# Attention scores with keys on partitions: weights no longer transposed, row sums on VectorE, heads chained

## The reference

```
scores = einsum('bqhd,bkhd->bhqk', q, k) / sqrt(64)
bias   = F[q] - F[k]                    # F = cumsum(log_sigmoid(f)), one row for each head
logits = where(key <= query, scores + bias, -inf)
y_b    = einsum('bhqk,bkhd->bqhd', softmax(logits), v)
gates  = sigmoid(x @ w_gate + b)        # 3 * 1024 columns, computed beside the attention
```

## Time and profile before

| | us |
|---|---|
| median of 3 runs | 1965.41 |
| profiled execution | 1961.69 |
| its span, first to last instruction | 1960.3 |
| TensorE busy with matmuls | 1913.3 (98%) |
| VectorE busy | 1124.5 (57%) |
| ScalarE busy | 706.6 (36%) |
| GpSimd busy | 435.0 (22%) |

### The profile page before, as it was taken

How to read it: one execution, slowest core, us unless ns; L and a number is a source line. 1 busy time by engine, 2 the same in 40 slices (tenths; PEclk the granted TensorE clock), 3 DMA queues, 4 the chain that set the end, 5 groups by cost and what they waited for, 6 DMA issues and landing times. The chain is left out here.

```text
span 1960.3 us, 30528 instructions
## 1 busy us (share of the span) xinstructions
PE 1913.3 (98%) x10560; PEld 1623.1 (83%) x10560; DVE 1124.5 (57%) x2133; ACT 706.6 (36%) x1081; POOL 435.0 (22%) x548
## 2 busy tenths in 40 slices
PE   7999999999999999999999999999999989999998
PEld 6878887888887888888888788888888878999997
DVE  4564235654245655646465665565645568777776
ACT  3121013021034555555555655455555541111110
POOL 2927930498000000000000000000000002222322
PEclk9999999999999999999999999999999989999999
DMA  7124225322432151231423515133142276555542
GB/s 190 67 86 118 86 86 196 63 107 107 139 109 93 49 139 54 80 110 47 138 68 87 175 48 139 62 87 109 49 128 66 91 251 209 170 173 171 174 118 86
DMA packets 103479, 221.68 MB, mean 113 GB/s; under 512 B 10936, under 2 KB 56680, under 8 KB 99816
## 3 DMA queue, kind: packets, MB, share of 16 engines
q1 hardware_dynamic: 89648, 161.41, 26.2%
q0 software_dynamic: 12608, 55.19, 10.1%
q10 hardware_dynamic: 1152, 4.19, 0.5%
HBM read 155.09 MB, written 65.08 MB: 112 GB/s over the span
## 5 line engine op out<-in xcount | busy, mean ns | idle before, releaser
L1386 PE MATMUL g_ps<-x_hi,w_lo 128*128 128x512 f32 x768 | 309.4, 403 | 0.0
L1386 PE MATMUL g_ps<-x_hi,w_hi 128*128 128x512 f32 x768 | 308.4, 402 | 0.0
L1302 DVE TENSOR_TENSOR pt_lo<-t_ps,pt_hi 128x512 fp32r<-128x512 f32 (+2 forms) x320 | 190.4, 606 | 138.2 <-ACT pt_hi L1208 137.8
L643 PE MATMUL tile_ps<-x_hi,w_hi 128*128 128x512 f32 x752 | 234.1, 393 | 11.2 <-DVE x_lo L362 11.2
L643 PE MATMUL tile_ps<-x_hi,w_lo 128*128 128x512 f32 x752 | 232.1, 390 | 0.0
L643 PE MATMUL tile_ps<-x_lo,w_hi 128*128 128x512 f32 x752 | 232.0, 390 | 0.0
L1386 PE MATMUL g_ps<-x_lo,w_hi 128*128 128x512 f32 x768 | 225.9, 410 | 3.9 <-PEq L1423 2.6
L1208 ACT ACTIVATE pt_hi<-t_ps 128x512 fp32r<-128x512 f32 (+2 forms) x320 | 170.4, 533 | 142.4 <-PE t_ps L1345 137.9
L1240 DVE CUSTOM_DVE_ANT_0 s_sb<-s_ps,f_row 128x512 f32<-128x512 f32 (+2 forms) x320 | 181.6, 604 | 35.1 <-PE s_ps L1334 34.4
L1116 POOL DMA_DIRECT2D mixT<-y_out x63 | 33.8, 536 | 748.1 <-DVE y_out L1254 748.1
L1345 PE MATMUL t_ps<-ident,s_sb 128*128 128x128 f32 x1088 | 172.1, 273 | 9.6 <-DVE pt_lo L1302 5.2
(11 more groups left out here) (276 smaller groups left out, 3537.4 us busy)
## 6 DMA issues: line engine op xcount, KB each, us to landing
w_lo_raw<-in_w_tiles SPq DMA_DIRECT2D x96, 512.0 KB, 3.6
gateT<-g_out SPq DMA_DIRECT2D x96, 256.0 KB, 3.0
gate<-gateT SPq DMA_DIRECT2D x64, 384.0 KB, 4.5
x_lo_raw<-in_xT SPq DMA_DIRECT2D x24, 512.0 KB, 8.4
qkvT<-zout SPq DMA_DIRECT2D x24, 512.0 KB, 3.2
silT<-zout SPq DMA_DIRECT2D x16, 512.0 KB, 2.7
k_ll<-qkvT POOLq DMA_DIRECT2D x16, 512.0 KB, 6.7
q_st<-qkvT POOLq DMA_DIRECT2D x16, 512.0 KB, 8.7
```

The lines of the kernel that those rows point to most:

```text
L643: last = pe.matmul(tile_ps[par][:, c * BANK:(c + 1) * BANK], w[par][:, k, :], x[:, k, c * BANK:(c + 1) * BANK], start=(k == 0 and j == 0), ...
L1302: dve.tensor_tensor(pt_lo[part], t_ps[n % 2][:, 0:keys].rearrange("p (k q) -> p k q", q=P), pt_hi[part].bitcast(F32), ALU.subtract).then_i ...
L1386: mm = pe.matmul(g_ps[c][:], w[j % 2][:, k, :], x[:, k, c * BANK:(c + 1) * BANK], start=(r == 0), stop=(r == 3 * KT - 1))
```

## The change

The block of 512 queries takes the place of the query tile, and keys are on partitions from the start. A head has 20 units (`UNITS`): query block b (0 to 3) and a pair of key tiles i; a diagonal unit has fewer columns.

- `scores_t` computes logits with the key tile as weight and up to 512 queries as moving operand, in two products: `k_hh` by `q_st`, and `kl2` by `q2`. `kl2` is the low part of k with four rows of ones beneath it; `q2` is the high part of q with four rows that hold minus the row's maximum, so the maximum is subtracted by the product. F[k] is now a bias of each partition (`neg_f`) of ScalarE's exponential, which reads PSUM and writes `p_raw`. A second set of 16 mask products for each head belongs to it.
- The maxima come from a separate pass, `score`, with queries on partitions as before but with one product (`q_st` by `k_hh`), 40 pieces for a head, with its 16 masks. VectorE runs the same custom instruction over them, in place in PSUM (`score_max`), and reduces four tiles at once; `max_row` transposes the maxima and `max_rows` writes them to `q2`.
- There are no transposes of weights. ScalarE and VectorE split `p_raw`, in SBUF, to `p_hi` and `p_lo`.
- Row sums: VectorE adds up `p_raw` over the key tiles in `acc` (`accumulate`), and `row_sums` does four plain float32 products with a column of ones for each query block; then the inverse and its transposes as before.
- `values` has 512 columns for each product in place of 256.
- Heads are chained: the product passes of the next head's blocks 0 and 1, its maxima, half of its v and its first unit are computed in the last steps of this one (`SCORE_STEPS`, `bank_uses`); keys and queries are split in steps 13, 15, 17 and 19. The first head does this work in `AHEAD`, with 32 fills. Scores, maxima, v, sums and inverses share two PSUM banks, `s_ps`.
- In the last head the split of the merge's first operand lies in the last steps; one copy of the head's code more stands in the program (first, phase 0, phase 1, last).

```diff
+UNITS = [(b, i) for b in range(4) for i in range(2 * b + 2)]
+SCORE_STEPS = {0: (14, (2, 2)), 1: (16, (1, 2, 2, 3)), 2: (0, (3, 4, 3, 2)), 3: (4, (2, 4, 3, 2, 3, 2))}
+MAX_STEP = {0: 16, 1: 0, 2: 4, 3: 10}
+V_STEP = {0: 16, 1: 2}
+SPLIT_STEP = (13, 15, 17, 19)
+FILL = (20, 13, 12, 15, 15, 13, 11, 16, 14, 13, 11, 9, 10, 17, 11, 17, 13, 18, 14, 17)
+FILL_TAIL = (3, 3, 3)
+FILL_AHEAD = (14, 10, 8)
...
         @block.scalar
+            def weights(at, n, first, ahead=0):
+                for s, k, q0 in tiles(n):
+                    act.wait_ge(st_full, at(2 * STEPS, 2 * (n + ahead * STEPS) + s + 1))
+                    act.activation(p_raw[n % 2][:, s, q0:], st_ps[:, s, q0:], ACT.Exp,
+                                   bias=neg_f[:, bass.ds(at(Q_TILES, k + ahead * Q_TILES), 1)]).then_inc(p_ready, 1)
...
+                if full(n):
+                    act.activation(p_hi[n % 2][:], p_raw[n % 2][:], ACT.Copy).then_inc(p_high, 1)
...
         @block.vector
-                    dve.tensor_tensor_reduce(s_sb[t % 2][:, k0:k0 + keys], s_ps[n % 3][:, 0:keys],
-                                             f_row[:, k0:k0 + keys], 1.0, -3e38, ALU.subtract, ALU.max,
-                                             mx[t % 2][:, j:j + 1]).then_inc(s_free, 1)
+                scores = s_ps[u % 2][:, 0:keys]
+                dve.tensor_tensor_reduce(scores, scores, f_row[:, j * BANK:j * BANK + keys],
+                                         1.0, -3e38, ALU.subtract, ALU.max, mx[:, t % 4, j:j + 1]).then_inc(s_free, 1)
...
+                        dve.wait_ge(accumulated, at(ACC, done + s))
+                        dve.tensor_tensor(a[:, q0:], a[:, q0:], p[:, s, q0:], ALU.add).then_inc(accumulated, 1)
...
+                if full(n):
+                    dve.tensor_tensor(lo[:], raw[:], hi[:].bitcast(F32), ALU.subtract).then_inc(p_low, 1)
...
         @block.tensor
-                    pe.matmul(ps, q_st[:, t * P:(t + 1) * P], k_hh[:, k0:k0 + keys], start=True, stop=False)
-                    last = pe.matmul(ps, q_st[:, t * P:(t + 1) * P], k_ll[:, k0:k0 + keys], start=False,
-                                     stop=not last_piece)
...
-                    for a in range(keys // P):
-                        last = pe.transpose(t_ps[n % 2][:, a * P:(a + 1) * P],
-                                            s_sb[t % 2][:, k0 + a * P:k0 + (a + 1) * P], ident[:])
...
+            def score(at, u, t, j, ahead):
+                ps = open_bank(at, u)
...
+                last = pe.matmul(ps[:, 0:keys], q_st[:, t * P:(t + 1) * P], k_hh[:, k0:k0 + keys], start=True,
+                                 stop=not diagonal)
+                if diagonal:
+                    last = pe.matmul(ps[:, keys - P:keys], ident_b[:], mask[:], start=False, stop=True)
...
+            def row_sums(at, u, b):
+                ps = open_bank(at, u)
+                pe.wait_ge(accumulated, at(ACC, acc_to(LAST_UNIT[b])))
+                for t in range(4):
+                    last = pe.matmul(ps[:, t:t + 1], acc[b % 2][:, t * P:(t + 1) * P], ones[:], start=True, stop=True)
...
+                    pe.matmul(ps, k_hh[:, keys], q_st[:, q], start=True, stop=False)
+                    last = pe.matmul(ps, kl2[:, keys], q2[:, q], start=False, stop=not diagonal)
+                    if diagonal:
+                        last = pe.matmul(st_ps[:, s, q0:q0 + P], mask[:], ident_b[:], start=False, stop=True)
...
+                pe.wait_ge(p_low, at(STEPS, n + 1))
+                for s, k, q0 in tiles(n):
+                    for j, p in enumerate((p_hi, p_lo)):
+                        last = pe.matmul(o_ps[b % 2][:, q0:], v_st[:, k, :], p[n % 2][:, s, q0:],
+                                         start=(k == 0 and j == 0), stop=(k == 4 * b + 3 and j == 1))
...
+                for n in range(STEPS):
+                    if n + 1 < STEPS:
+                        rows = AHEAD_USES + index.get(("max", UNITS[n + 1][0]), 0) + 1
+                        scores_t(at, n + 1, at(HEAD_USES, rows), first)
...
+                    fill((n, 0))
+                    for a, use in enumerate(bank_uses(n, last)):
...
+                        fill((n, a + 1))
...
+                    values(at, n, first, index)
```

More of the change, by code:

```diff
@@ new lines, with tiles, full, score_pieces @@
+FILL = (20, 13, 12, 15, 15, 13, 11, 16, 14, 13, 11, 9, 10, 17, 11, 17, 13, 18, 14, 17)
+FILL_TAIL = (3, 3, 3)
+FILL_AHEAD = (14, 10, 8)
+HEAD_USES, AHEAD_USES = 54, 15
+Y_STEP = STEPS - 4
+def tiles(n):
+    b, i = UNITS[n]
+    return [(s, 2 * i + s, max(0, 2 * i + s - 4 * b) * P) for s in range(2)]
+def full(n):
+    b, i = UNITS[n]
+    return i < 2 * b
+def score_pieces(b):
+    return [(t, j) for t in range(4 * b, 4 * b + 4) for j in range(b + 1)]
+def bank_uses(n, last):
+    uses = [("max", b) for b, step in MAX_STEP.items() if step == n and not (last and b == 0)]
+    for b, end in enumerate(LAST_UNIT):
+        uses += [("sum", b)] * (n == end + 1) + [("inv", b)] * (n == min(end + 2, STEPS))
+    uses += [("v", half) for half, step in V_STEP.items() if step == n and not (last and half == 0)]
+    for b, (first, share) in SCORE_STEPS.items():
+        if 0 <= n - first < len(share) and not (last and b < 2):
+            done = sum(share[:n - first])
+            uses += [("score", t, j) for t, j in score_pieces(b)[done:done + share[n - first]]]
+    return uses
@@ L955, in fill_plan @@
-    splits["start"].append(1)
-    for n, s in enumerate(slots):
+    slots, counts = [], {}
+    for a, n in enumerate(FILL_AHEAD if first else ()):
+        slots.append(("ahead", a))
+        counts["ahead", a] = n
+    for n in range(STEPS):
+        here = FILL[n] - (first and (1 if n else FILL[0] - 8))
+        parts = len(bank_uses(n, False)) + 1
+        for a in range(parts):
+            slots.append((n, a))
+            counts[n, a] = here * (a + 2) // (parts + 1) - (here * (a + 1) // (parts + 1) if a else 0)
@@ L957, in fill_plan @@
+    for a, n in enumerate(FILL_TAIL):
+        slots.append((STEPS, a))
+        counts[STEPS, a] = n
+    slots_total = sum(counts.values())
+    counts[STEPS, len(FILL_TAIL) - 1] += total - slots_total
+    assert counts[STEPS, len(FILL_TAIL) - 1] >= 0
+    ends, splits, done = {s: [] for s in slots}, {n: [] for n in range(STEPS)}, 0
+    splits[0].append(1)
+    for s in slots:
         before, done = done, done + counts[s]
@@ L1021, in stage_attend @@
+                "p_high", "p_low", "accumulated", "v_high", "v_done", "o_low_ready", "o_sum"))
         kq_loaded, v_loaded, f_loaded = kept.kq_loaded, kept.v_loaded, kept.row_loaded
-        def pieces(t):
-            n0 = sum(-(-(a + 1) // 4) for a in range(t))
-            keys = (t + 1) * P
-            return [(n0 + j, j * BANK, min(BANK, keys - j * BANK)) for j in range(-(-keys // BANK))]
-        def splits(slot, last):
-            return [j for j in w_splits[slot] if not (last and j == G_TILES)]
@@ L1033, in pieces_to, with acc_to, splits, heads @@
-        def pieces_to(t):
-            return pieces(t)[-1][0] + 1
+        acc_ops = [len(tiles(n)) - (full(n) and UNITS[n][1] == 0) for n in range(STEPS)]
+        ACC = sum(acc_ops)
+        def acc_to(n):
+            return sum(acc_ops[:n + 1])
+        def splits(plan, n, last):
+            return [j for j in plan[2][n] if not (last and j == G_TILES)]
+        def heads(eng, before, body):
+            before(0)
+            body(lambda k, c: c, lambda k, c: c, True, False)
+            for phase in range(2):
+                if phase:
+                    before(phase)
+                with eng.Fori(1 - phase, PHASE_HEADS - phase) as i:
+                    body(lambda k, c: i * k + (c + phase * PHASE_HEADS * k), lambda k, c: i * k + c, False, False)
+            body(lambda k, c: (HEADS - 1) * k + c, lambda k, c: (PHASE_HEADS - 1) * k + c, False, True)
@@ L1226, in _ @@
+            heads(act, before, body)
         @block.vector
@@ L1320, in _ @@
+            heads(dve, before, body)
         @block.tensor
         def _(pe):
[L1322 to L1335 removed]
```

658 lines of the change are left out of this document (387 added, 271 removed).

## The result

The changed kernel takes 1988.14 us (median of 4 runs, 1985.53 to 1990.88) beside 1965.24 for the kernel before on the same chip: ratio 1.0117, interval 1.0099 to 1.0136. Beside later experiments it was 1989.67, ratio 1.0134 [1.0117, 1.0151]. The forecast was 1945 us: it came out slower, and above the range.

What follows compares the result with a forecast made beforehand. TensorE was taken as the bound (98% busy); instructions -24, waits -12, coarse grain +4, start +6 and phases +6 gave -20 us, so 1965.4 - 20 = 1945 us, with an 8-in-10 range of 1915 to 1980.

Steps and rivals of the forecast that it cites:

- row sums: a pass at 0.065 us: TensorE, 32 blocks: 256 plain float32 passes priced like a 64-column transpose, +19 us; +31 at the far end.
- pass for the maxima: 8.0 us a head: TensorE: the separate score products for the row maxima, +64 us over 8 heads.
- all other instructions (a remainder): TensorE: weight transposes -120 us, `values` -6, inverse rows -3, `scores_t` 0 with new masks +16, `max_row` +6.
- waits that go: TensorE's two waits a head for the exponentials of long rows disappear: 16 x 0.72, -12 us.
- coarse grain: Allowance of 0.5 us a head, +4 us, bounds 0 and 3 us a head.
- start of the first head: TensorE waits for banks while VectorE works through score pieces and splits: +6 us, bounds 3 and 10.
- between the phases: New head's step 0 work on VectorE queues behind 16 splits of reloaded x: +6 us, bounds 2 and 12.
- Nothing is late in its place if VectorE keeps up: Steady heads: exponentials start early enough; VectorE busy 91 of TensorE's 117 us, in no step the longer.
- VectorE as the bound through a custom instruction of 1.2 us: Writing to PSUM doubles each score piece's cost: 1993 us; chance 0.21, including waits of several us a head.
- The mild form: Handshake over two banks alone costs 3 us a head: 1965 us; within the 0.21 for VectorE-bound or waits.
- The rival of the small instructions: Row sums (+12) and starts (+10) at their far ends eat the gain: about 1965 us; no gain, chance 0.12.
- The change does not do what it says: Waits for the exponential merely move to `values`, TensorE waiting for `p_low` in each unit; no chance of its own.

Runs made afterwards that it cites:

- experiment 4: Changed kernel without the 128 masks in the product pass for the maxima: 1980.6 us, ratio 1.008 to the kernel before.
- experiment 6: Changed kernel with ScalarE's and VectorE's head loops written out, accumulation of full units cut to 16 of 512 columns: 1979.24 us, ratio 1.0082.
- experiments 1 and 2: ScalarE's and VectorE's loops over heads written out, in the changed kernel (1979.99 us, ratio 1.0083) and in the kernel before (1963.09 us, ratio 0.9998).
- experiment 8: Changed kernel with those loops written out, custom instruction writing bfloat16 to SBUF instead of back to PSUM: 1977.74 us, ratio 1.0074.
- b3: Changed kernel, loops written out; first head: a fill behind each of the start's last eight score pieces, VectorE's last key/query split in step 1: 1976.9 us.
- experiment 3: Changed kernel with one four-column row-sum product per query block replacing four one-column ones (inverse rows wrong): 1978.43 us, ratio 1.0073.

## Why the prediction was wrong

The forecast was a sum of -20 us; `stage_attend` gave +24.3. The 44 us between, from starts of TensorE in a steady head:

| step of the prediction | forecast | measured | difference |
|---|---|---|---|
| row sums: a pass at 0.065 us | +19 | 0.81 us for the eight passes of a block (seven distances of 0.112) and 0.09 behind them, +29 | +10 |
| pass for the maxima: 8.0 us a head | +64 | 8.62, +69 | +5 |
| all other instructions (a remainder) | -107 | -97: a head without its waits went from 119.05 to 119.14, +1 in 8 heads, less the two rows above | +10 |
| waits that go -12, coarse grain +4 | -8 | +1.3 a head, +10; heads entered without a jump -2 | +16 |
| start of the first head | +6 | +11 | +5 |
| between the phases | +6 | 5.4 before, 10 after, +4.5 | -1.5 |

Start and seam are what is left beside eight steady heads of 121.88 us, so they stand for the last head too, which has no next one to prepare.

- *Transposes, values, scores.* Right: transposes, with the fill behind each group, are 11.7 + 2.9 us a head (117 in all, forecast 120), `values` went from 16.9 to 16.1, `scores_t` took 16.9 where `queries` took 17.3. The mask was priced too high: 0.08 us in experiment 4, forecast 0.13.
- *Row sums: the first step that failed, by its size.* I took the price from the v transposes, whose weights have 64 rows. The weight loads of the changed kernel tell it apart (PEld, the row sums' and then the v transposes'):

```profile
866.49 1.09 PEld L1547 LDWEIGHTS s_ps<-ones,acc 128*128 128x128 f32 x8
```

```profile
887.26 0.57 PEld L1539 LDWEIGHTS s_ps<-ident,vT 64*128 64x128 f32 x8 [0.37 <-issue]
```

  The row sums' passes start 0.112 us apart, at the pace of their loads (the first load, at 866.49, lies ahead of them, beside a fill). The v transposes' loads come every (0.57 - 0.14) / 7 = 0.06, although 64 columns move in each of them. The nearest row of before was the one with 128 rows, not the one with few columns. The Trainium skill's figure ("TensorE: Matmul & The Clock Gate", section "LDWEIGHTS (loading the stationary operand)"), some 107 ns for 128 columns, agrees with 0.112 here. That the rows do not matter, as the section says, is not what these rows show: weights of 64 rows and 128 columns come every 0.06 us. No run changes the rows alone.
- *"Nothing is late in its place if VectorE keeps up": the second, and larger, failure.* The two waits of a head went (1.46 us; only one of them was for the exponential, the other for `pt_lo`), and I asked of VectorE only whether each step's busy time was below TensorE's. It was (91.4 us of 121.9), and experiment 6 shows that a tenth less work for it, taken elsewhere, changes nothing. What I did not ask is in which place of its queue the instruction stands that a bank waits for, and when. Three places cost 2.74 us a head: the reciprocal behind three splits, `max_rows` behind the jump, v behind ScalarE's copy. The jump's part, 1.8 us in four heads, was no step of mine at all; experiments 1 and 2 show it.
- *The first head.* The direction was right and the size short by 5: between the half clock (0.50 from 627 to 639) and the hole of 3.3 us after 630.57. Part of it is the clock, which I had at full speed, but b3, with 0.86 there, took only 3 us off the first head.
- *The rivals.* VectorE as the bound through a custom instruction of 1.2 us is refuted: it takes 0.70 us (after L1361: 699 ns), and in experiment 8 its destination changes that by 9 ns (and the read behind it by 55). The mild form, a handshake over the banks of 3 us a head, came near in size (2.74 us of waits a head), but most of it was not the banks' handshake: it was what stood ahead of three instructions, the jump above all. The rival of the small instructions came in part: row sums +10 where it had +12, the start +5. I held these two apart, each with its chance, and both came; together, at 20 each above the forecast, they would have given 1985. That this is near 1988 is in part luck, since +10 of the measured sum is a remainder that neither of them names.
- *"The change does not do what it says".* It does: the long exponential wait is gone, and TensorE does not wait ahead of `values` in a steady head.

Open: whether an order exists in which no wait is left, and the +10 of the other instructions. A fill's mean distance, waits left out, went from 0.241 to 0.244 us, which is 6 us in 2304 fills; the rest is not put on a cause.

## What to carry over

Busy shares below the bound say only that an engine can keep up, not that it does: for each wait put down what stands ahead of the releasing instruction in its engine's order, what its loop does before it, and when the engine gets there. Price a product by the row whose weights have the same shape, rows and columns. When a saving pays only half, look which waits have grown before looking for a bound: in experiment 3 two had grown, in experiment 4 none, and there the price was wrong. Moving the work that stood ahead of both waits made the saving of 21 us pay 20; with that order kept, but the score pieces ahead of it gone, it paid 18.

## What was not expected of the hardware

- VectorE stands for 2.29 to 2.50 us at the back edge of its loop over heads, four times in this stage, and ScalarE for 2.49 and 2.31 us at two of them (at the other two its next work waits for a DMA); with the loops written out TensorE's wait of 1.87 us behind it is gone.
- A product with one moving column in plain float32 repeats every 0.112 us with weights of 128 x 128; transposes whose weights are 64 x 128 every 0.06.
- A reciprocal of 64 x 512 takes 3.35 us where a subtraction takes 0.68; one of 128 x 4 takes 0.18.
- Reading the accumulator behind the custom instruction takes VectorE 138 ns where that instruction wrote to PSUM (44.2 us in 320) and 83 where it wrote to SBUF (26.4 us).
- TensorE's clock fell to 0.50 at the start of a stage and at the seam, after stretches with gaps (12.1 us busy of 15 at the start).
